# A hybrid decoder step on one core: the state-free half of all chunks moved to a front stage, with the 32-blocks of the inverses made by substitution on GpSimd

## The reference

```
decay = exp(where(tril, gc[i] - gc[j], -inf))          # gc: cumulated log decays
A     = I + where(strict, (beta*k) k^T * decay, 0)     # unit lower triangular
u, w  = solve(A, [beta*v, beta*k*exp(gc)])
qk    = (q k^T) * decay
# scan over chunks, state S (128x128 per head):
v_new = u - w S
o     = (q*exp(gc)) S + qk v_new
S     = S*g_last + (k*exp(gc[-1]-gc))^T v_new
```

## Time and profile before

| stretch, us | what runs | PE busy | granted clock |
|---|---|---|---|
| 0 to 367.5 | input block | 336.85 | 0.98 |
| 367.5 to 410.5 | mixer, chunk 0 | 36.02 | 0.74 |
| 410.5 to 707.8 | chunks 1 to 7 | 275.53 | 0.99 |
| 707.8 to 791.4 | samples, end of the mixer | 72.05 | 0.90 |
| 791.4 to 1600.4 | FFN | 792.00 | 0.99 |

### The profile page before, as it was taken

One profiled execution on the slowest core, in us unless ns is written; L12 is line 12 of the kernel. 1 busy time (PEld: TensorE's weight loads), 2 busy tenths in 40 slices (PEclk: granted clock), 3 DMA queues, 4 the chain that ended last, 5 costly groups with the idle time before them and its releaser, 6 DMA issues.

```text
span 1600.4 us, 22345 instructions
## 1 busy us (share of the span) xinstructions
PE 1512.5 (95%) x8667; PEld 1367.8 (85%) x8667; DVE 724.0 (45%) x1150; ACT 351.3 (22%) x569; POOL 132.9 (8%) x200
## 2 busy tenths in 40 slices
PE   5999999997999999999899999999999999999997
PEld 3799899996777777776699998989898999989895
DVE  5346554534666666665333333242323333332415
ACT  5353522331111111111221111102020211112012
POOL 1000000001222222220000000000000000000001
PEclk9999999997999999999899999999999999999999
DMA  6012122262122221112350201101010101010002
GB/s 196 14 43 71 67 92 91 80 194 95 40 66 66 66 66 55 54 64 86 115 212 27 79 26 52 52 26 52 26 52 26 61 24 72 26 52 26 0 0 111
DMA packets 52561, 105.11 MB, mean 66 GB/s; under 512 B 4785, under 2 KB 30321, under 8 KB 52529
## 3 DMA queue, kind: packets, MB, share of 16 engines
q1 hardware_dynamic: 52528, 104.67, 19.0%
HBM read 82.66 MB, written 22.00 MB: 65 GB/s over the span
## 4 chain that ended last, share of the span: by engine, by line
PE 45%; issue 2%; ACT 2%; DVE 1%; DMA 1%; POOL 0%; DVEq 0%; ACTq 0%; POOLq 0%
PE bank L87 15%; PE bank L89 15%; PE bank L88 15%; ACT gu_hi L1591 1%; DMA out_y<-y_out 1%; DVE acc L1677 0%; DVE y_out L1641 0%; DVE hf L1653 0%; ACT y_out L1627 0%; POOL fstat L1692 0%; DVEq L1676 0%; ACTq L76 0%; POOL fstat L1690 0%; POOLq L1509 0%; DVE gu_lo L1634 0%
## 5 line engine op out<-in xcount | busy, mean ns | idle before, releaser
L1653 DVE TENSOR_TENSOR hf<-sg,bank 128x364 f32<-128x364 f32 (+1 forms) x66 | 35.1, 532 | 344.7 <-PE bank L89 342.6
L87 PE MATMUL bank<-ht_hi,w_hi 128*128 128x364 f32 (+1 forms) x576 | 190.2, 330 | 0.0
L89 PE MATMUL bank<-ht_hi,w_lo 128*128 128x364 f32 (+1 forms) x576 | 189.5, 329 | 0.0
L88 PE MATMUL bank<-ht_lo,w_hi 128*128 128x364 f32 (+1 forms) x576 | 189.4, 329 | 0.0
L87 PE MATMUL bank<-ht_hi,gu_first_hi 128*128 128x364 f32 (+1 forms) x528 | 174.1, 330 | 1.4 <-PEq L843 1.4
L88 PE MATMUL bank<-ht_lo,gu_first_hi 128*128 128x364 f32 (+1 forms) x528 | 174.0, 330 | 0.0
L89 PE MATMUL bank<-ht_hi,gu_first_lo 128*128 128x364 f32 (+1 forms) x528 | 173.7, 329 | 0.0
L89 PE MATMUL bank<-ht_hi,gu_lo 128*128 128x364 f32 (+1 forms) x528 | 173.2, 328 | 0.0
L1677 DVE TENSOR_TENSOR acc<-acc,bank 128x512 f32<-128x512 f32 (+1 forms) x198 | 132.3, 684 | 90.3 <-PE bank L89 90.3
L87 PE MATMUL bank<-ht_hi,gu_hi 128*128 128x364 f32 (+1 forms) x528 | 173.1, 328 | 0.0
L88 PE MATMUL bank<-ht_lo,gu_hi 128*128 128x364 f32 (+1 forms) x528 | 173.1, 328 | 0.0
(11 more groups left out here) (265 smaller groups left out, 2385.1 us busy)
## 6 DMA issues: line engine op xcount, KB each, us to landing
w_raw<-in_w_in SPq DMA_DIRECT2D x24, 512.0 KB, 4.2
dn_raw<-in_w_down SPq DMA_DIRECT2D x22, 512.0 KB, 4.2
scratch_qkv<-cb_y SPq DMA_DIRECT2D x12, 512.0 KB, 2.7
qkv_in<-scratch_qkv SPq DMA_DIRECT2D x8, 768.0 KB, 6.3
gu_first_raw<-in_w_gate SPq DMA_DIRECT2D x11, 512.0 KB, 3.5
gu_first_raw<-in_w_up SPq DMA_DIRECT2D x11, 512.0 KB, 4.3
gu_raw<-in_w_gate SPq DMA_DIRECT2D x11, 512.0 KB, 3.6
gu_raw<-in_w_up SPq DMA_DIRECT2D x11, 512.0 KB, 4.3
```

Of the source, the lines that this page charges most:

```text
L87: pe.matmul(out, w_hi, x_hi, start=start, stop=False)
L88: pe.matmul(out, w_hi, x_lo, start=False, stop=False)
L89: return pe.matmul(out, w_lo, x_hi, start=False, stop=stop)
L1653: eng.tensor_tensor(hf[b][:, 0:m], sg[b][:, 0:m], psum[2 * b + 1][:, 0:m], ALU.mult).then_inc(hf_done, 1)
```

## The change

The mixer's order is new. A **front stage** goes through all nine tiles, the samples first, as unrolled code, and does all that needs no state: transposes, norms, decays, u and the masked q·k. For the prompt it keeps u, mq, v and the normalized k in the memory of ht_hi and ht_lo (`kept`), which is written only later. As each u is made, SP sends its four diagonal 32-blocks per head to DRAM (`su`), one block per row: 8 chunks x 4 heads x 4 blocks are 128 rows. Read back, one block lies in each partition, and POOL inverts all 128 at once by forward substitution, 31 steps of two instructions. Beside it the samples' states and their projection run. The inverses and their transposes go to DRAM (`sx`, `sxt`); per chunk eight small DMAs put them back as block-diagonal matrices `x32`, `y32` over zeros. The chunk then has two levels left (32 and 64) and the state's products. The samples come first (Tile.k is 0), so the residual of chunk c is normalized in chunk c+2 (`t2`), its projection done in c+1 (`t`). The chunk loop runs over pairs. Semaphores of the input block are cleared by POOL and used again.

```diff
@@ SP, front stage and the way back
-            def load_qkv(c):
...
+            for f in FRONTS[1:]:
+                c = f.c
+                eng.wait_ge(m_["a_u"], f.a + 1)
+                rows = scratch["su"][c * 4 * H:(c + 1) * 4 * H, :].rearrange("(h b) (j i) -> b j h i", b=4, i=BLOCK)
+                for b in range(4):
+                    lo = b * BLOCK
+                    eng.dma_start(rows[b], f.u[lo:lo + BLOCK, :, lo:lo + BLOCK]).then_inc(m_["dg_out"], 16)
+                if c + 3 < NC:
+                    eng.wait_ge(m_["a_qk"], f.a + 1)
+                    eng.dma_start(qkv_b[c % 3][:, :, :], chunk_of(scratch["qkv"], c + 3)).then_inc(q_ld[c % 3], 16)
...
+            eng.wait_ge(m_["dg_out"], 16 * 4 * NC)
+            eng.wait_ge(m_["s_ymm"], 2)
+            eng.dma_start(sub_u[:, :, :], scratch["su"].rearrange("p (j i) -> p j i", i=BLOCK)).then_inc(m_["su_ld"], 16)
...
+            eng.wait_ge(m_["sub_done"], 2)
+            for name, src in (("sxt", sub_u), ("sx", sub_x)):
+                eng.dma_start(scratch[name].rearrange("p (j i) -> p j i", i=BLOCK), src[:, :, :]).then_inc(m_["sub_out"], 16)
+            eng.wait_ge(m_["sub_out"], 32)
+            eng.wait_ge(m_["zero32"], 2)
+            load_xy(0)
+            load_slot(u_, FRONTS[1].u, "u_ld")
@@ PE, front stage (front: transposes and sums; products: k.k and k.q)
+            front(FRONTS[0])
+            decay(FRONTS[0])
+            for f in FRONTS:
+                nxt = FRONTS[f.a + 1] if f.a + 1 < MT else None
+                if nxt:
+                    front(nxt)
+                turn_k(f)
+                if nxt:
+                    decay(nxt)
+                products(f)
+                if 2 <= f.a <= 5:
+                    sample_level(f.a // 2, f.a % 2 == 0)
+            samples_states()
@@ PE, chunk(c, s, nth, t, t2): the order of its parts
-                for q in range(1, t.levels):
...
+                eng.wait_ge(m_["u_ld"], 16 * (c + 1))
+                eng.wait_ge(m_[f"xy_ld{s}"], 128 * nth)
...
+                        mm = eng.matmul(psum[2 + r][:, h * P:(h + 1) * P], u_[:, h, :], x32[s][:, h, :],
+                                        start=True, stop=True)
...
+                fill(rg_steps[0:2])
...
+                        mm = eng.matmul(psum[4 + r][:, h * P:(h + 1) * P], pp[:, h, :], y32[s][:, h, :],
+                                        start=True, stop=True)
...
+                        mm = eng.matmul(psum[6 + r][:, h * P:(h + 1) * P], y32[s][:, h, :], pp[:, h, :],
+                                        start=True, stop=True)
...
+                fill(rg_steps[2:5])
...
+                        mm = eng.matmul(psum[2 + r][:, h * P:(h + 1) * P], u_[:, h, :], x_[:, h, :],
+                                        start=True, stop=True)
...
+                if t2:
+                    turn_x(t2)
+                fill(rg_steps[5:6])
...
+                if t:
+                    turn_o(t, 2)
+                fill(rg_steps[6:8])
...
+                fill(o_steps[0:3])
...
+                fill(o_steps[3:7])
...
+                fill(o_steps[7:8])
@@ POOL, the substitution (step waits on sub_chain for each instruction)
+            xs = sub_x[:, :, :].rearrange("p i k -> p (i k)")
+            step(eng.memset(xs, 0.0))
+            step(eng.memset(xs[:, 0::BLOCK + 1], 1.0))
+            eng.wait_ge(m_["s_p"], 2)
+            eng.wait_ge(m_["su_ld"], 16)
+            for j in range(BLOCK - 1):
+                if j == MID:
+                    scale_o(Tile(NC))
+                rows, cols = BLOCK - 1 - j, j + 1
+                part = sub_t[:, 0:rows * cols].rearrange("p (i k) -> p i k", k=cols)
+                step(eng.tensor_tensor(part, sub_u[:, j, j + 1:].unsqueeze(2).to_broadcast([P, rows, cols]),
+                                       sub_x[:, j, 0:cols].unsqueeze(1).to_broadcast([P, rows, cols]), ALU.mult))
+                below = sub_x[:, j + 1:, 0:cols]
+                step(eng.tensor_tensor(below, below, part, ALU.subtract))
+            eng.tensor_copy(sub_u[:, :, :], sub_x[:, :, :].rearrange("p i k -> p k i")).then_inc(m_["sub_done"], 2)
```

More of the change, by code:

```diff
@@ L744, in mixer_block @@
     four = lambda name: B(name, [P, H, P])
+    x_at = B.at
     x_in = B("x_in", [P, D])
     xn = B("xn2", [P, D])
-    sq = xn[:, :].rearrange("p (t n) -> p t n", n=P)
[L748 to L754, removed]
@@ L784, in mixer_block @@
+    FRONTS = [Front(a) for a in range(MT)]
     class Tile:
@@ L833, in by_token, with chunks, two @@
         return flat(buf)[:, b * TS:(b + 1) * TS]
-    def mlow2(q, n):
-        return over(mlow[q][0:n, 0:n], n)[:, 0:2]
     def pair_of(ap, n, r, m=P):
         return ap[0:n, 2 * r:2 * r + 2, 0:m]
+    def chunks(run, last):
+        run(0, 0, 1, None, Tile(NC))
+        run(1, 1, 1, Tile(0), None)
+        def two(j):
+            for s in range(2):
+                run(2 * j + s, s, j + 1, Tile(2 * j + s - 1), Tile(2 * j + s - 2))
+        with last.Fori(1, NC // 2) as j:
+            two(j)
+    END, BEFORE_END = Tile(NC - 1), Tile(NC - 2)
     with nc.Block() as block:
@@ L1110, in _, with first_products @@
+                fill(o_steps[3:7])
+                eng.wait_ge(m_["mq_ld"], 16 * (c + 1))
+                for h in range(H):
+                    mm = eng.matmul(psum[5][:, h * P:(h + 1) * P], mq[:, h, :], vnew[:, h, :], start=True, stop=True)
+                mm.then_inc(m_["o2_mm"], 1)
+                fill(o_steps[7:8])
+            chunks(chunk, eng)
+            def first_products(q):
+                m = GROUPS[0][1]
                 for f in range(KT):
@@ L1189, in spread_samples, with square_o @@
                                    ACT.Copy, scale=scale).then_inc(m_["spread_done"], 1)
-            chunk(0, None)
-            with eng.Fori(1, NC) as c:
-                chunk(c, Tile(c - 1))
-            chunk(NC, Tile(NC - 1))
-            end = Tile(NC)
-            square_o(end)
+            split_rg(Tile(NC))
+            eng.wait_ge(m_["s_w"], 1)
+            for h in range(H):
+                spread_samples(h)
+            def square_o(t):
+                eng.wait_ge(m_["o_done"], t.k + 1)
+                if not t.samples:
+                    eng.wait_ge(m_["on_tr"], t.k)
+                eng.activation(on[0:t.n, :, :], o_[0:t.n, :, :], ACT.Square, scale=1.0 / P).then_inc(m_["osq_done"], 1)
@@ L1387, in _ @@
+            chunks(chunk, eng)
+            sum_o(END)
+            norm_x(BEFORE_END)
+            norm_o(END)
+            for half in range(2):
+                split_x(BEFORE_END, half)
+            mix(END, 4)
+            mix_low(END)
             eng.wait_ge(gu_first_done, 1)
@@ L1446, in zero_spreads @@
[L1446 to L1458 removed]
+            eng.wait_ge(m_["a_qk"], MT)
@@ L1459, in mixer_block @@
+            root_x(BEFORE_END)
+            scale_o(END)
+            root_x(END)
+            numbers = sorted(sem.num for sem in k["done_with"])
+            for n in numbers:
+                if n - 1 not in numbers:
+                    last = next(m for m in itertools.count(n) if m + 1 not in numbers)
+                    eng.sem_clear(range(n, last + 1))
     return (gu_first_raw, gu_first_hi, gu_first_lo), (k["after_wo"], at)
```

1113 lines of the change are left out of this document (636 added, 477 removed).

## The result

The changed kernel takes 1515.39 us (median of 4 runs, 1512.54 to 1519.14) beside 1601.78 for the kernel before (1599.78 to 1602.91): ratio 0.9461, 95% interval 0.9446 to 0.9477. It is 86 us faster; the prediction had 50 (1550, range 1521 to 1587).

What follows compares the result with a forecast made beforehand. PE was taken to bound the mixer's chunk loop. Terms 367.5 + 73.5 + 9 + 53 + 12 + 22 + 173.5 + 30.5 put the FFN's start at 741 instead of 791.6 us, so 1550.7 us, range 1521 to 1587.

Steps and rivals of the forecast that it cites:

- The chunk period: Loop over chunks 1 to 7: 24.5 us per chunk, 171.5 for seven, bounds 22.5 and 29.3.
- With 10% for gaps (15% now): 24.5: Chunks 1 to 7: PE's list of 22.1 us raised by 10% for gaps to a period of 24.5.
- The 2 us for the clock's rise: Chunks 1 to 7: 2 us added to 171.5 for the clock rising, making 173.5.
- The front: Front stage, nine iterations before the substitution: 73.5 us, bounds 62 to 100.
- I take 8.0 for the five iterations that reload: Front stage: 8.0 us for each of five iterations, as pieces go ahead of the qkv load on the same engines.
- Chunk 0: First prompt chunk, without projection to fill it and at 1.2 GHz: 22 us; at full clock 14.
- The substitution: POOL's 31 steps inverting the diagonal blocks, with slowing by DVE: 53 us, lower bound 42 if POOL is never held.
- Rival 1: Substitution: POOL pays 77 ns per short inner run, 76 us in all, time 1627; chance 0.08.
- Rivals 2 and 3: Chunks keep 7.2 us of waits, 1585, chance 0.13; front bound by loads, 1571, chance 0.08; both together about 1605, 0.04.
- Rival 4: All at the low bounds: front 62, substitution 42, chunks 22.5; 1514, put at 1522 as samples set the end; chance 0.09.
- the double cost per packet: Diagonal pieces' 128-byte DMA runs: if each packet cost double, the sum would be 10 us longer; not adopted.
- The tail: From the last chunk to the FFN's first matmul: 30.5 us, with PE idle for 4; no gain expected.

Runs made afterwards that it cites:

- pe_more: Changed kernel with the output product of query and state issued twice in each chunk; 1521.17 us, ratio 0.9489.
- dve_more: Changed kernel with VectorE repeating the multiplication before both first-level mask operations of each chunk; 1516.39 us, ratio 0.9472.
- fills_last: Changed kernel with a chunk's 16 projection steps all behind its last product instead of between its products; 1542.28 us, ratio 0.9634.
- handover: Changed kernel with later samples' stop, earlier loads, reordered way to chunk 0 and tail, plus VectorE taking over the substitution at step 18; 1492.25 us.
- half_steps: Changed kernel with the substitution stopped after 16 of its 31 steps, inverses incomplete; 1495.89 us, ratio 0.9348.
- load_first: Changed kernel with the front's load of the chunk three on ahead of the four stores of diagonal pieces; 1513.24 us, ratio 0.9444.
- lock_two: Changed kernel with eight more VectorE subtractions of 64x512, both operands in SBUF, during the substitution; 1515.28 us, one run.
- lock_wide: Changed kernel with VectorE repeating four times a 64x1024 expansion, both operands in SBUF, during the substitution; 1518.82 us, one run.
- lock_one: Changed kernel with eight more VectorE subtractions of 64x512, second operand in PSUM, during the substitution; 1516.25 us, one run.
- warm: Changed kernel with 90 added identity products on PE behind the samples' projection, before chunk 0; 1514.26 us, ratio 0.9446.

## Why the prediction was right in kind and short in size

1. *The chunk period* (17.4 of the 34.5 us). PE's list of 22.1 us was right: the period is 22.43. The failed step is "With 10% for gaps (15% now): 24.5". I had placed each wait against the list and found only nw late, by 0.35; it was late by 0.17. Then I overrode this by an average over the chunk of the kernel before. Nearly half of the 7 us in that average belonged to what was removed: four levels below 32, whose chain through DVE's transposes held PE for 0.45 us each, and PE's wait of 1.4 for the level that DVE made alone; of the rest a part stood in stretches without projection. pe_more, dve_more and fills_last show it: the loop stretches with PE, not with DVE, and only because the projection stands between the products. The 2 us for the clock's rise were not there either: the first chunks' clock was 1.00.
2. *The front* (6.8). The failed step is "I take 8.0 for the five iterations that reload". In the changed kernel these tiles recurred after 6.8 to 7.7 us, 36.2 for the five instead of 40; with the load ahead of the pieces after 6.5 at most. I had priced the load at 6.3, it took 5.2, and the pieces landed in 1.5 instead of the 3.0 of the nearest row. That the loads bind at all was right, by 1.7 us of waits and, in half of the profiles with this order, some 2 of clock.
3. *Chunk 0* (5.8). I priced it wholly at the half clock, 22; the windows show 0.83, and the clock was at 1.00 from 508.8 us on, after 0.54 in the first 6 us. My price at full clock, 14, agrees with handover's 14.1.
4. *The substitution* (1.1 off) agrees in total, by luck: three terms are off and cancel. POOL stood still for 4.2 us, a stall that I had put only into the case of late samples; DVE stretched POOL's operations by 7.9 us where I had 11 (the stretched operations less the unhindered ones of the same size); and what is left of the 51.9 is 39.8 where I had 42. half_steps shows it on the path one for one.
5. *Rivals.* Rival 1 is out: the first step's 31 runs of one element took 0.24 us. The Trainium skill, "GPSIMD Engine Reference", section "Performance pitfalls for Q7 kernels", tells of about 102 cycles for each small read command; that a run of one element is such a command does not fit this trace. Rivals 2 and 3 are out by the period and by the waits of 1.7 us. Rival 4, all at the low bounds, came nearest and holds for one of its three terms: the period is at its bound of 22.5, the front's 66.7 lies between its bound and mine, and the substitution was not at 42. I gave it 0.09 and a time of 1522, with the samples setting the end, which they did not (they end at 480.1, POOL at 492.3). The Trainium skill, "DMA: Bandwidth & Descriptors", section "Specifications", wants 512 bytes per transfer for line rate; the double cost per packet that I tried for it would have added 10 us to the sum, and pieces of 128-byte runs at 1.5 and 1.8 us show no sign of it.
6. *The tail* was right (30.5 and 31.5), with its wait of 4 measured at 3.3.

## What to carry to other kernels

Where a stage is priced by PE's list, add the waits that you can name, each against the work that stands beside it; a share of waiting taken from the old loop goes with the instructions that caused it, and here nearly half of it did. Short waits can go with a loss of more than their length, as the clock may fall behind them: the changed kernel's front, with 1.7 us of waits for loads, was 4.0 longer than load_first's. A chain on one slow engine is shortened by handing it to another in the middle, but what stands behind it in that engine's list then waits for it, as the samples' norm does in handover.

## What the runs showed of the hardware

- GpSimd and VectorE slow each other while both read two SBUF operands. Beside a row of VectorE operations one GpSimd operation was stretched per VectorE operation, by 0.35 us beside those of 0.68 (lock_two) and by 0.86 beside those of 1.22 (lock_wide), where VectorE's own took 1.60 each. With VectorE's second operand in PSUM GpSimd lost nothing (10.21 us with and without, lock_one). The Trainium skill, "SBUF — State Buffer", section "SBUF: two separate sides", tells of an exclusive lock on the port pair that the two share, held for a whole instruction by whichever starts first; one stretched operation per VectorE operation fits that, but for some 0.35 us of each VectorE operation that GpSimd does not lose.
- A dependent operation on GpSimd costs 0.31 us for 31 elements, from start to start (440.45 to 440.76 us in the changed kernel); on VectorE 0.22 (474.47 to 474.69 us in handover).
- The clock can fall to 1.2 GHz behind a gap as well as in it: in warm PE stood still from 502.1 to 504.1 us at a clock of 1.00, and 506.1 to 508.1 ran at 0.50 with PE busy throughout; in the changed kernel's longer gap before chunk 0, PE idle from 480.3 us, the clock was 1.00 up to 484 us and 0.50 from 486 on.
